# One encoder layer on one core: the low-rank product in column groups, and a new order ahead of the first expert pair

## What is computed

```python
h = rms_norm(x) * (1 + sc1) + sh1              # sh1, sc1, g1, ... from silu(c) @ w_mod + b_mod
z = h @ w_in
u_pool, q, k, v, g, r_f, r_b = split(z)        # r_f, r_b: 16 columns each, the low-rank gates
la_f = log_sigmoid(r_f @ w_gk_up[0] + b_gk[0]) / 16     # la_b likewise
mix = concat(pool_mixer(u_pool), gla_mixer(q, k, v, g, la_f, la_b)) @ w_out
x = x + g1 * mix
h = rms_norm(x) * (1 + sc2) + sh2
s = sigmoid(h @ w_router)                      # 32 experts in 4 groups
# the best group by the sum of its two best scores, then its two best experts;
# weights = their scores divided by the sum of the two
x = x + g2 * sum_over_two_experts(weight * (silu(h @ w1[e]) * (h @ w3[e])) @ w2[e])
return rms_norm(x) * final_g
```

## Time and profile before

| | us |
|---|---|
| median of 3 runs | 738.73 (737.96 to 739.45) |
| span of the profiled execution | 736.0 |
| PE busy | 683.0 (93%) |
| DVE busy | 345.1 (47%) |
| ACT busy | 175.0 (24%) |
| POOL busy | 55.5 (8%) |
| DMA | 259.41 MB, mean 352 GB/s |

### The profile page before, as it was taken

The page is one execution under the profiler, slowest core; times in us unless marked ns, Lnnn a source line. Parts: engine busy times, 40 slices in busy tenths (PEclk is TensorE's granted clock), DMA queues, the critical chain, the costliest instruction groups (busy, mean ns, idle before and its releaser), DMA issues.

```text
span 736.0 us, 8999 instructions
## 1 busy us (share of the span) xinstructions
PE 683.0 (93%) x3686; PEld 375.2 (51%) x3686; DVE 345.1 (47%) x630; ACT 175.0 (24%) x310; POOL 55.5 (8%) x55
## 2 busy tenths in 40 slices
PE   3799999999998999999999989779999999998893
PEld 2478787876877634344344344233443444443442
DVE  3554978798977313333333343132333333331336
ACT  4333468323333121111011021100110210210104
POOL 2006800100000100000000000000000000000000
PEclk9899999999999899999999999888999999999997
DMA  9996345665369599999999999999999999999962
GB/s 334 389 383 247 115 157 215 232 228 229 115 248 416 197 422 420 428 424 429 425 424 428 425 428 426 427 426 426 425 427 426 428 425 428 427 428 425 427 258 114
DMA packets 39497, 259.41 MB, mean 352 GB/s; under 512 B 4190, under 2 KB 4574, under 8 KB 26272
## 3 DMA queue, kind: packets, MB, share of 16 engines
q1 hardware_dynamic: 34992, 250.11, 82.9%
q0 software_dynamic: 2688, 4.88, 1.8%
q10 hardware_dynamic: 1776, 3.84, 1.4%
HBM read 259.20 MB, written 4.19 MB: 358 GB/s over the span
## 4 chain that ended last, share of the span: by engine, by line
PE 79%; DMA 13%; DVE 6%; issue 1%; ACT 1%; SPq 1%; DVEq 0%; POOLq 0%
PE bank L924 27%; PE bank L628 19%; PE bank L933 12%; DMA ring<-in_w 8%; PE bank L941 3%; PE bank L942 3%; DMA ring<-in_w_in 3%; PE bank L896 2%; DMA xg_rows<-x_rows,keep 1%; DVE x L1707 1%; PE bank L949 1%; PE bank L840 1%; PE bank L748 1%; PE bank L904 1%; PE bank L580 1%
## 5 line engine op out<-in xcount | busy, mean ns | idle before, releaser
L924 PE MATMUL bank<-ring,low 128*64 128x512 f32 x928 | 228.0, 599 | 5.6 <-DMA ring<-in_w 4.7
L924 PEld LDWEIGHTS bank<-ring,low 128*64 128x64 f32 x928 | 74.3, 138 | 121.8 <-issue 121.8
L1707 DVE TENSOR_TENSOR x<-x,bank 128x512 f32<-128x512 f32 x136 | 84.4, 683 | 79.0 <-PE bank L942 77.2
L933 PE MATMUL bank<-ring,low 128*64 128x512 f32 x432 | 113.3, 595 | 0.9 <-DVE x L1707 0.9
L933 PEld LDWEIGHTS bank<-ring,low 128*64 128x64 f32 x432 | 35.3, 137 | 66.1 <-issue 64.4
L1697 DVE SCALAR_TENSOR_TENSOR y_raw<-bank,keep,g2b 128x512 f32<-128x512 f32 x32 | 24.0, 751 | 87.3 <-PE bank L933 87.3
L1764 DVE TENSOR_TENSOR low<-low,bank 128x512 f32<-128x512 f32 x16 | 11.0, 688 | 106.4 <-PE bank L924 106.4
L941 PE MATMUL bank<-y_hi,slot_tok 128*128 128x512 f32 x128 | 53.5, 418 | 0.2 <-DVE y_lo L1702 0.2
L1334 ACT COPY low<-bank 128x512 f32<-128x512 f32 x16 | 9.4, 585 | 172.6 <-PE bank L904 172.6
L942 PE MATMUL bank<-y_lo,slot_tok 128*128 128x512 f32 x128 | 50.3, 393 | 0.0
L1864 POOL DMA_INDIRECT xg_rows<-x_rows,keep x17 | 16.9, 996 | 413.6 <-PE bank L896 355.5
(11 more groups left out here) (252 smaller groups left out, 904.2 us busy)
## 6 DMA issues: line engine op xcount, KB each, us to landing
ring<-in_w SPq DMA_DIRECT2D x84, 2048.0 KB, 23.9
ring<-in_w_mod SPq DMA_DIRECT2D x11, 2048.0 KB, 12.3
mid<-in_w SPq DMA_DIRECT2D x11, 2048.0 KB, 23.1
ring<-in_w_in SPq DMA_DIRECT2D x4, 2048.0 KB, 21.5
ring<-in_w SPq DMA_DIRECT2D x8, 1024.0 KB, 8.3
ring<-in_w_out SPq DMA_DIRECT2D x2, 2048.0 KB, 10.4
x<-in_x SPq DMA_DIRECT2D x4, 512.0 KB, 5.9
mid<-in_w_mod SPq DMA_DIRECT2D x1, 2048.0 KB, 21.3
```

The source lines that it names most:

```text
L924: last = mm(bk[e * CAP:(e + 1) * CAP, :], xb[:, k, e * CAP:(e + 1) * CAP], unit(n % SLOTS, KD)[:, k, :], start=k == 0, stop=k == KD - 1)
L933: last = mm(bk[e * CAP:(e + 1) * CAP, :], hid_t[:, k, e * CAP:(e + 1) * CAP], unit(n % SLOTS, KF)[:, k, hf * 512:(hf + 1) * 512], start=k ...
L1707: return v.tensor_tensor(acc[:, t, c], acc[:, t, c], bk[:, :], ALU.add)
```

## The change

The low-rank product becomes 16 fp32 matmuls in four column groups: eight chunks, each with the high and the low part of h, with the 32 real columns of the unsplit weights. The four partial sums stay in four groups of 32 partitions; ACT copies all 128, and the up matrix is loaded four times, so that the gate products add the groups up. `wr_hi`, `wr_lo`, `wr_raw` and POOL's wait for them go.

For the first pair, the one-hot matrix no longer waits for the routing weights. PE forms the two row columns first, DVE the row numbers, and POOL may gather. Only then DVE normalises the weights, cuts them into parts and has PE form the three weight columns. The reciprocal and scaling of the weights also move behind the rank line. The fillers ahead of the first pair change from 7, 5, 42 to 7, 14, 8, 8.

Unit 5 waits for `h2_saved`.

```diff
--- before.py
+++ after.py
@@ -54,6 +54,7 @@
 RING = 8
 SLOTS = 9
 PRE_SLOTS = 4
+LAST_RING = 5
 UPP = 6
 XPAIR = 7
 XUNITS = 3
...
@@ -326,8 +324,9 @@
         wpool = low[:, 2048:2560].rearrange("p (g c) -> p g c", g=4)
         cb = low[:, 2560:2816].rearrange("p (k m) -> p k m", k=KD)
         masks = low[:, 2816:3072]
-        wup = low[0:2 * RANK, 3072:3584].rearrange("p (d c) -> p d c", d=2)
-        r_t = low[0:2 * RANK, 3584:4096]
+        wr = low[:, 0:KD * P].rearrange("p (k c) -> p k c", k=KD)
+        wup = low[:, 3072:3584].rearrange("p (d c) -> p d c", d=2)
+        r_t = low[:, 3584:4096]
         h2t = low[:, :].rearrange("p (k t) -> p k t", k=KD)
         xg = low[:, 512:2560].rearrange("p (b k s) -> p b k s", b=2, k=KD)
         sil = low[:, 2560:3072]
...
@@ -494,6 +494,9 @@
                 elif n == PRE_SLOTS:
 
                     sp.wait_ge(job_done, JOB["wo13"] + 1)
+                elif n == LAST_RING:
+
+                    sp.wait_ge(h2_saved, 16 * NT)
                 elif n == MIDDLE:
 
                     sp.wait_ge(job_done, JOB["hT31"] + 1)
@@ -631,9 +634,13 @@
             def low_rank():
 
                 b = start("r")
-                pe.wait_ge(wr_parts, 1)
+                pe.wait_ge(wr_in, 16)
                 for k in range(KD):
-                    last = three(b[:, :], h_hi[:, k, :], h_lo[:, k, :], wr_hi[:, k, :], wr_lo[:, k, :], k, k == KD - 1, True)
+                    for i, x_ in enumerate((h_hi, h_lo)):
+                        n = 2 * k + i
+                        j = n % 4
+                        last = mm(b[32 * j:32 * j + 32, :], wr[:, k, 0:2 * RANK], x_[:, k, :].bitcast(F32), start=n < 4,
+                                  stop=n >= 2 * KD - 4, tile_position=(0, 32 * j), skip_group_check=True)
                 last.then_inc(job_done, 1)
 
             def product(unit_name, names, a_hi, a_lo, stationary_w, ready=None):
@@ -669,7 +676,7 @@
             low_rank()
             product("qk", ["q0", "q1", "k0", "k1"], h_hi, h_lo, True)
             read_out(pe, "r")
-            pe.wait_ge(small_in, 48)
+            pe.wait_ge(small_in, 96)
             for i in range(4):
                 b = start(f"gk{i}")
                 mm(b[:, :], wup[:, i // 2, (i % 2) * P:(i % 2 + 1) * P], r_t, start=True, stop=True).then_inc(job_done, 1)
@@ -904,15 +911,24 @@
                     last = nc.tensor.transpose(TB[:, k * P:(k + 1) * P], by_k[:, k, :], ident)
                 return last
 
-            def slots_to_partitions():
+            def columns_to_partitions(c):
 
                 for e in range(2):
                     for t in range(NT):
-                        mm(A1[e * CAP:(e + 1) * CAP, 0:5], onehot[:, t, e * CAP:(e + 1) * CAP],
-                           pair_cols[:, t, e, :], start=t == 0, stop=t == NT - 1)
+                        last = mm(A1[e * CAP:(e + 1) * CAP, c], onehot[:, t, e * CAP:(e + 1) * CAP],
+                                  pair_cols[:, t, e, c], start=t == 0, stop=t == NT - 1)
+                return last
+
+            def slots_turned():
+
                 for t in range(NT):
                     last = nc.tensor.transpose(slots_bank[:, t * P:(t + 1) * P], onehot[:, t, :], ident_b[:, :])
                 return last
+
+            def slots_to_partitions():
+
+                columns_to_partitions(slice(0, 5))
+                return slots_turned()
 
             def up_product(n0, xb, w):
                 bk = (A1, A3)[w]
@@ -972,13 +988,16 @@
             pe.wait_ge(ident_rounded, 1)
             unread(7, Y0)
             pe.wait_ge(p_ready, 1)
-            slots_to_partitions().then_inc(pt_psum, 1)
-            unread(5, Y0)
+            columns_to_partitions(slice(3, 5)).then_inc(first_row, 1)
+            slots_turned().then_inc(pt_psum, 1)
+            unread(14, Y0)
+            pe.wait_ge(first_weights, 1)
+            columns_to_partitions(slice(0, 3)).then_inc(first_weights_psum, 1)
+            unread(8, Y0)
             pe.wait_ge(p_ready, 2)
             pe.wait_ge(pt_ready, 1)
-            pe.wait_ge(w_ready, 1)
             slots_to_partitions().then_inc(pt_psum, 1)
-            unread(42, Y0)
+            unread(8, Y0)
             turn(0)
 
             def extra_begin(j):
@@ -1156,8 +1175,9 @@
             mod_copy(1)
             high_parts(4, 6)
             mod_copy(3)
-            act.dma_start(wr_raw, A["wr"]).then_inc(wr_in, 16)
-            act.dma_start(wup.rearrange("p d c -> p (d c)"), A["wup"]).then_inc(small_in, 16)
+            act.dma_start(wr.rearrange("p k c -> p (k c)"), A["wr"]).then_inc(wr_in, 16)
+            for j in range(P // (2 * RANK)):
+                act.dma_start(wup[2 * RANK * j:2 * RANK * (j + 1), :, :].rearrange("p d c -> p (d c)"), A["wup"]).then_inc(small_in, 16)
             read_out(act, "mcol1")
             mixed(4)
             high_parts(6, 7)
@@ -1177,7 +1197,7 @@
                 o, left, _ = POOL_AT[g]
                 nc.scalar.copy(up[:, o + left:o + left + S], b[:, :]).then_inc(out_scalar, 1)
             b = full(act, "r")
-            nc.scalar.copy(r_t, b[0:2 * RANK, :]).then_inc(out_scalar, 1)
+            nc.scalar.copy(r_t, b[:, :]).then_inc(out_scalar, 1)
             high_parts(12, 20)
             for i, name in enumerate(("q0", "q1", "k0", "k1")):
                 b = full(act, name)
@@ -1428,10 +1448,6 @@
             high_and_low(6)
             low_weights(7, 8)
             high_and_low(7)
-            dve.wait_ge(wr_in, 16)
-            link(v.tensor_copy(wr_hi[:, :, :].rearrange("p k c -> p (k c)"), wr_raw))
-            v.tensor_tensor(wr_lo[:, :, :].rearrange("p k c -> p (k c)"), wr_raw,
-                            wr_hi[:, :, :].rearrange("p k c -> p (k c)").bitcast(F32), ALU.subtract).then_inc(wr_parts, 1)
             def mod_steps(n0, n1):
 
                 for n in range(n0, n1):
@@ -1504,7 +1520,7 @@
                 ins.then_inc(out_vector, 1)
 
             dve.wait_ge(att_zero, 1)
-            dve.wait_ge(small_in, 48)
+            dve.wait_ge(small_in, 96)
             for d in range(2):
                 for h in range(HEADS):
                     b = full(dve, f"att{d}{h}")
@@ -1644,22 +1660,15 @@
             link(v.tensor_tensor(gview(rt_a), goh4, rt_oh1.unsqueeze(2).to_broadcast(big4), ALU.mult))
             v.tensor_copy(chosen_b, rt_a).then_inc(chosen, 1)
 
-            link(v.tensor_tensor(gwt[:, :, 0:E_N], rt_a, rt_s, ALU.mult))
-            link(v.tensor_reduce(rt_m, gwt[:, :, 0:E_N], AX_X, ALU.add))
-            link(v.reciprocal(rt_m, rt_m))
             weights = gwt[:, :, 0:E_N]
-            link(v.tensor_tensor(weights, weights, rt_m.unsqueeze(2).to_broadcast([P, NT, E_N]), ALU.mult))
+            link(v.tensor_tensor(weights, rt_a, rt_s, ALU.mult))
+            link(v.tensor_reduce(rt_m, weights, AX_X, ALU.add))
             b = full(dve, "rk")
             v.scalar_tensor_tensor(rankm[:, :, 0:E_N], b[:, 0:NT * E_N].rearrange("p (t e) -> p t e", t=NT), 1.0, rt_a,
                                    ALU.add, ALU.mult).then_inc(out_vector, 1)
             b = full(dve, "cnt")
             v.tensor_copy(held, b[:, 0:E_N]).then_inc(out_vector, 1)
             dve.wait_ge(out_vector, len(OUT_VECTOR))
-            for i in range(3):
-                link(v.tensor_copy(w_parts[:, :, 0:E_N, i], weights))
-                if i < 2:
-                    link(v.tensor_tensor(weights, weights, w_parts[:, :, 0:E_N, i], ALU.subtract))
-
 
             A1, A3, TB, Y0, Y1, G0, G1, CA = bank
             SUM_BANKS = (TB, CA, Y0, Y1)
@@ -1667,10 +1676,11 @@
             BLOCK_BANKS = (A1, A3, TB, CA, G0, G1, Y1, Y0)
             iota8 = iota.unsqueeze(1).to_broadcast([P, NT * 2, CAP])
 
-            def one_hot(ranks, weights, off, cols_ready, cols_count):
+            def one_hot(ranks, parts, off, cols_ready, cols_count):
 
                 v.tensor_scalar(rank_pair, ranks, off, None, ALU.add).then_inc(cols_ready, 1)
-                v.tensor_copy(pair_cols[:, :, :, 0:3], weights)
+                if parts is not None:
+                    v.tensor_copy(pair_cols[:, :, :, 0:3], parts)
                 dve.wait_ge(cols_ready, cols_count)
                 return v.tensor_tensor(onehot[:, :, :].rearrange("p t (e s) -> p (t e) s", e=2),
                                        rank_pair.rearrange("p t e -> p (t e)").unsqueeze(2).to_broadcast([P, NT * 2, CAP]),
@@ -1681,10 +1691,18 @@
                 e = slice(2 * q, 2 * q + 2)
                 return one_hot(rankm[:, :, e], w_parts[:, :, e, :], 0.0, rank_cols, q + 1).then_inc(p_ready, 1)
 
+            def weight_column(buf):
+
+                return v.tensor_reduce(w_slot[:, buf:buf + 1], A1[:, 0:3], AX_X, ALU.add)
+
+            def row_column(buf):
+
+                return v.tensor_scalar(row_of[:, buf:buf + 1], A1[:, 3:4], A1[:, 4:5], float(S), ALU.add, ALU.add)
+
             def to_columns(buf):
 
-                v.tensor_reduce(w_slot[:, buf:buf + 1], A1[:, 0:3], AX_X, ALU.add)
```

(25 more changed lines are left out.)

## The result

The changed kernel takes 735.71 us (median of 6 runs, 733.75 to 736.88), the kernel before 739.06 (6 runs, 737.74 to 740.26): a ratio of 0.9949, 95% interval 0.9933 to 0.9966. The forecast was 734.9 with a range of 733.0 to 738.7. The number holds; the sum behind it does not, as the rows show.

The account below looks back on a forecast made before the run. The prediction took the second half's full DMA stream as the bound, started by the first pair's up product. Span 736.0 less 1.6 (low-rank product) and 2.2 (earlier up product) gave 732.2, plus 2.73: 734.9 us, range 733.0 to 738.7.

Parts of the forecast that it names:

- The bound: Second half is a full DMA stream; a microsecond earlier at the first pair's up product is one at the end.
- Part 1: Low-rank product: 16 column-grouped fp32 matmuls take 3.84 us instead of 5.44, gaining 1.60, all reaching the first pair.
- Part 2's front: Ahead of the first pair: one-hot 1.83 us earlier, row numbers near 238.65, gather starting at 239.5, 3.3 earlier.
- Part 3: Unit 5 behind the row stores: stores land by 237.5, unit 5 and the gather beside it at 246.1.
- Rival 1: Row stores not cleared: gather still starts at 242.78, product at 249.1, total 735.7 us; chance 0.15.
- A second condition ends later: the list: First up product waits for VectorE's list of extra blocks, done at 248.3, so it starts 2.2 us earlier than 250.47.
- the price of the gap: PE idles from 244.6 to 246.1 before turning; the forecast still allowed 1.8 us from turning to product.
- rival 2: Clock falls on the first up product: 6.9 us at half level costs 3.4, total 738.3; 740.1 if longer; chance 0.17.
- the prediction's own first sign of being wrong: First up product: the forecast is wrong if the granted clock is at half there.
- the 2.73 us: Time by which the median of runs, 738.73, lay above the profiled span of 736.0, carried over unchanged.
- rival 3: Low-rank column groups don't overlap: product takes 14.5 us, total 745.6; decided at 0.48 us per matmul; chance 0.05.
- Rival 4: After the first pair, some later wait takes the lead back, total 738.7 us; chance 0.08.

Follow-up runs that it names:

- 34-filler execution: Changed kernel with 34 fillers in place of the last 8 ahead of turning the first rows; 735.11 us, again 734.89.
- unit 5 free: Changed kernel without unit 5's wait for the row stores, so it is issued with the other two units; 738.57 us, ratio 1.0004.
- gather first: Changed kernel with unit 5 also waiting for the first gather, PE's list wait moved to the seventh pair, 10 last fillers for 8; 735.78 us.
- unit 5's wait without the order: Kernel before with the grouped low-rank product and unit 5 waiting for the row stores, without the new PE and VectorE order; 736.00 us.

## Why the prediction was right in its number and wrong in its sum

**The bound** held. C is constant to within 1.3 us wherever the same units were still to be sent, so to within that a microsecond at SP's first half unit is a microsecond at the end, with the exception at the end of one 34-filler execution. But I put the condition at the wrong place: I counted from the *start* of the first up product, while slots come free as it *advances*. The two differ when the clock falls on it.

**Part 1** was right in mechanism and undersized: 1.60 forecast, 2.24 measured in A (177.05 - 174.81). Of this 1.87 is the low-rank product itself (5.44 - 3.57; 0.223 a matmul, where the row I took had 0.24), 0.20 the gates, which I had costed at no change, and the remaining 0.17 is not placed. ACT's three more DMA issues cost nothing, as said: its idle time before the row is still 3.40.
The Trainium skill ("TensorE: Matmul & The Clock Gate", section "Why this matters for your kernels") has its 3.07 times for four tiles that split the rows of the array; carried over to column groups, as the prediction did, it gives 4.7 us for this product, an estimate from that page. The measurement decides: 14.5 / 3.57 is 4.1 times. The 0.91 behind the 14.5 comes from the gate products over 32 rows; with the 0.86 of those over 128 rows (3.43 / 4), as many as the grouped matmuls have, it is 3.8.

**Part 2's front** was right. After the count, the one-hot came at 0.89 us (234.39 - 233.50; forecast 237.24 - 236.13 = 1.11), the gather at 3.17 (forecast 3.37), released by the row numbers.

**Part 3** was right. The stores cleared 1.5 us after the count (235.0 - 233.50; forecast 237.5 - 236.13 = 1.4), and the gather landed with unit 5 at 10.3 (forecast 9.97). Rival 1 is out, and "unit 5 free" shows what it would have been: 738.57, not the rival's 735.7, since the clock falls there too. The two prices I used were right as well: a gather alone takes 4.3 ("gather first"; forecast 4.4), and unit 5 took the 8.6 forecast. That the gather ends with the unit held: it landed within 0.2 of it here, and within 0.3 in "unit 5's wait without the order", where unit 5 landed at 243.8 and the gather at 244.1.
The Trainium skill ("DMA: Bandwidth & Descriptors", section "Queues, rings and completion order") has each DMA engine take turns between the queues that it has work for. The page does not say which of two transfers ends first; the prediction drew that from it, and only the rows show it.

**"A second condition ends later: the list"** was nearly right and did not decide. The list was done 11.45 us after the count (244.95 - 233.50), against 12.17 forecast, and the product started at 13.04, because turning at half clock ended later. With the clock kept, the second 34-filler execution shows the forecast itself: the product is released by the list's last line, 12.01 after the count.

**The step that failed is the price of the gap.** The forecast had PE "free at 244.6 and waits for the gather", saw the idle time, and still priced the product at the full clock, giving the half clock a chance of 0.17 as rival 2. It happened in both profiles of the changed kernel and in both other kernels with the new order and 8 last fillers: the prediction's own first sign of being wrong. The gap was also mis-sized: 1.5 us forecast (244.6 to 246.1), 2.84 measured, mostly because PE was free 7.5 us after the count (241.0 - 233.50) and not 8.5. Rival 2's length was right, 6.9 us forecast and 6.8 measured, the window from 243.5 to 250.3; its price, 3.4, was too high. Turning cost 0.8 to 0.9 more (1.97 against 1.16 or 1.05 with 34 fillers), the part of the product that SP waits for 1.87 more: 2.7 to 2.8, since part of the stretch was idle time and issue.

So the sum was 736.0 - 1.60 - 2.2 = 732.2 and the measured span is 733.8: part 1 gave 0.64 more and the start of the kernel 0.39, and the order of parts 2 and 3, forecast at 2.2, cost 0.57. The half that SP waits for was done 5.55 after the product's start instead of 3.68 before the change, and that took back more than the 1.30 by which it started earlier relative to the count. In the runs the same stands as: part 1 alone 0.9972, parts 2 and 3 alone 1.0012, both 0.9949. The two multiply to 0.9984, which is at the edge of what the intervals cover; the medians (736.11 for part 1 alone, 735.71 and 736.17 for both) do not show that difference, and no row accounts for it.

That the median still came within 0.8 of the forecast is luck. The order fell short by 2.8 us; 1.0 of this came back by part 1 and the start, and 0.8 by the 2.73 us that the prediction carried from span to median. The profiled run of the changed kernel took 735.71 with a span of 733.8, only 1.9 apart: the 2.73 mixed the span of a quick execution with the median of others.

**Rivals 3 and 4.** The groups overlap, at 0.223 us a matmul against the 0.48 from which rival 3 decides; it is out. Rival 4, a later wait that takes the lead back, is not seen in the changed kernel (C 481.7 against 481.8), but is in "gather first" and in one 34-filler execution.

## What to carry to other kernels

When a change makes a wait end earlier, look at what filled that wait. Fillers sized for the old landing either hold the engine (as 42 did with an early gather) or, cut too far, leave a gap after which the granted clock is at half on the work that matters; size them so that they end when the data lands. Where a stream is the bound, sending a transfer early while the DMA engines are idle can be worth as much as starting the work early, and moving it behind something to speed that thing up can give the same time back, as "gather first" did. And measure between events of the same execution (here A, B, C): A repeats within 0.13 us in eight executions and B within 0.06 in the changed kernel's two, where whole spans differ by 2. They do not repeat so well across a stretch at half clock of varying length (B, 18.02 and 17.50 with the same order) or at the end of the stream (C, 485.9 and 482.6 with the same kernel).

## What was not expected of the hardware

- Sixteen column-grouped fp32 matmuls of 512 columns with 32 columns of weights took 3.57 us, 0.223 each, in all eight executions, against 0.91 or 0.86 (3.43 / 4, over 128 rows) for an ungrouped one: 3.8 to 4.1 times.
- The four gate products over 128 rows take 3.43 us where the same four over 32 rows took 3.63.
- A gap of 2.70 to 4.29 us ahead of turning came with the half clock in all four executions that had one, and a gap of 0.25 or none did not in three. In the order of before, a gap of 1.55 or 1.56 and shorter ones came with it in all three executions. Near the end of the kernel gaps of about 2 us came with it in seven executions (1.97 in "gather first", then 8.78 for the product) and not in three (the changed kernel: 2.16 and 2.58, then 7.09 each time). So the length of one gap alone does not tell.
- The start of the low-rank product varies from 57.66 to 59.55 between executions, nearly 2 us. The changed kernel and its versions with 34 fillers have the same program up to there, and even these four range from 57.82 to 59.55.
